# Modulation sums along rows on VectorE, and a start that follows the rows of h one by one, in a three-block transformer kernel

## What is computed

```
shift, scale, gate = split(c @ mod_w[layer, 0] + mod_b[layer, 0], 3)
h = rms_norm(x, norm_w[layer, 0, 0]) * (1 + scale) + shift
y = mixer(h)                         # or swiglu(h)
x = x + gate * rms_norm(y, norm_w[layer, 0, 1])
```

## Time and profile before

| | us |
|---|---|
| median of 3 runs | 1029.87 (1028.25 to 1030.72) |
| span of the profiled execution | 1029.8 |
| TensorE / VectorE / ScalarE busy in it | 987.3 / 792.3 / 559.9 |

### The profile page before, as it was taken

How to read it: one execution, slowest core, us unless ns; L and a number is a source line. 1 busy time by engine, 2 the same in 40 slices (tenths; PEclk the granted TensorE clock), 3 DMA queues, 4 the chain that set the end, 5 groups by cost and what they waited for, 6 DMA issues and landing times. The chain is left out here.

```text
span 1029.8 us, 21353 instructions
## 1 busy us (share of the span) xinstructions
PE 987.3 (96%) x8118; PEld 954.4 (93%) x8118; DVE 792.3 (77%) x1320; ACT 559.9 (54%) x1126; POOL 4.6 (0%) x14
## 2 busy tenths in 40 slices
PE   6999989999999999999999999999999999999996
PEld 5998768999999999989899999998989899999995
DVE  4758996788888777888788888876767857887775
ACT  2435774644444455574554444445657457666763
POOL 0100000000000000000000000000000000000000
PEclk9999999999999999999999999999999999999998
DMA  9995677488888656813558888774722425555431
GB/s 359 348 271 184 246 269 254 168 309 299 306 306 304 247 185 233 304 57 121 186 217 315 300 301 308 282 262 167 248 66 68 155 80 195 200 197 184 183 115 41
DMA packets 62569, 227.59 MB, mean 221 GB/s; under 512 B 7042, under 2 KB 7298, under 8 KB 62244
## 3 DMA queue, kind: packets, MB, share of 16 engines
q1 hardware_dynamic: 61716, 224.02, 60.5%
q0 software_dynamic: 640, 2.10, 0.9%
q10 hardware_dynamic: 144, 0.52, 0.1%
HBM read 225.04 MB, written 1.57 MB: 220 GB/s over the span
## 5 line engine op out<-in xcount | busy, mean ns | idle before, releaser
L1994 PE MATMUL bank<-hH,wH 128*128 128x258 f32 (+1 forms) x1544 | 444.2, 288 | 12.1 <-DVE hL L1343 8.4
L1995 PE MATMUL bank<-hL,wH 128*128 128x258 f32 (+1 forms) x1544 | 438.0, 284 | 0.0
L1996 PE MATMUL bank<-hH,wL 128*128 128x258 f32 (+1 forms) x1544 | 436.3, 283 | 0.0
L1278 DVE TENSOR_TENSOR wL<-raw,wH 128x1024 fp32r<-128x1024 f32 x270 | 327.9, 1220 | 43.9 <-ACT wH L813 42.8
L1994 PEld LDWEIGHTS bank<-hH,wH 128*128 128x128 f32 x1544 | 292.4, 189 | 20.0 <-issue 11.2
L813 ACT ACTIVATE wH<-raw 128x1024 fp32r<-128x1024 f32 x270 | 276.3, 1047 | 46.8 <-DMA raw<-in_weights 25.0
L1996 PEld LDWEIGHTS bank<-hH,wL 128*128 128x128 f32 x1544 | 293.6, 190 | 0.0
L1995 PEld LDWEIGHTS bank<-hL,wH 128*128 128x128 f32 x1544 | 293.1, 190 | 0.4
L1994 PE MATMUL bank<-aH,wH 128*128 128x256 f32 x592 | 169.2, 286 | 3.0 <-DVE wL L1278 3.0
L1996 PE MATMUL bank<-aH,wL 128*128 128x256 f32 x592 | 168.6, 285 | 0.0
L1995 PE MATMUL bank<-aL,wH 128*128 128x256 f32 x592 | 168.5, 285 | 0.0
(11 more groups left out here) (353 smaller groups left out, 1138.6 us busy)
## 6 DMA issues: line engine op xcount, KB each, us to landing
raw<-in_weights SPq DMA_DIRECT2D x270, 512.0 KB, 4.6
modbuf<-in_mod_w SPq DMA_DIRECT2D x69, 512.0 KB, 6.1
modbuf<-in_w_ada SPq DMA_DIRECT2D x36, 512.0 KB, 6.5
strips<-in_mod_w SPq DMA_DIRECT2D x16, 512.0 KB, 7.0
strips<-in_w_ada SPq DMA_DIRECT2D x12, 512.0 KB, 7.0
strips<-bias_table POOLq DMA_DIRECT2D x8, 256.0 KB, 6.8
raw<-in_mod_w SPq DMA_DIRECT2D x2, 512.0 KB, 4.2
otok<-in_mod_w SPq DMA_DIRECT2D x2, 512.0 KB, 9.8
```

The source lines that it names most:

```text
L1278: V.tensor_tensor(wL[:, slot, :], raw[:, slot, :], wH[:, slot, :].bitcast(F32), ALU.subtract).then_inc(lo_ready[c], 1)
L1994: mm(out, lhs_h, rhs_h, start=start, stop=False, skip_group_check=True)
L1995: mm(out, lhs_h, rhs_l, start=False, stop=False, skip_group_check=True)
L1996: return mm(out, lhs_l, rhs_h, start=False, stop=stop, skip_group_check=True)
```

## The change

- A matrix of a job is now laid out by output column: partition = output feature, 1024 input features along the row. `c` lies in `crow`, the same row on all 128 partitions. A job is one `tensor_tensor_reduce` on VectorE: product with `crow`, sum along the row, times a weight (the norm weight), starting from bias (times weight). Its result is one column of `mv`, `sc1` or `gw1`, ready for use. The start values of all columns are set in five small operations at the beginning. A second instruction per job reads the sum out.
- `mod_sum` and `mod_take` are gone, with their semaphores; users wait for a number of jobs (`wait_mods`). The accumulators are gone.
- `keep_clock` behind the norm sums is 18 matmuls in all four gaps (it was 3, 3, 6 and 3, beside 16, 16, 8 and 16 of sums).
- `silu(c_2)` is taken of the whole row, 128 x 1024, by ScalarE at the end of `f0`.
- In the start the order of SyncE is: parameters, first half of `x`, `crow`, second half, then matrices in pairs (scale and shift of row k), with units 0, 1 and 2 among them and unit 3 behind. `first_rows(k)`, `first_high(k)` and `first_low(k)` make row k of `h` once its two sums are there, and TensorE does `first_products` of units 0, 1, 2 for that row. Five of the eight shift sums stay on TensorE (`shift_product`), from matrices in the old layout. The gates come before `bc` and the values. The strips wait for the last row of `h`.
- The loops of SyncE and VectorE over steps of the feed-forward phases are written out.

```diff
+SHIFT, SCALE, GATE = range(3)
+MODS = [(0, part * KT + k) for k in range(KT) for part in (SCALE, SHIFT)]
+ON_TENSOR = [2 * k + 1 for k in (1, 3, 5, 6, 7)]
...
-            dst = acc[:, at:at + D]
-            cc = cvec[:, 0, :] if m < 4 else csil[:, :]
-            if d >= 1:
-                eng.wait_ge(mod_used, d)
-            if k == 0:
-                ops.tensor_scalar(dst, src, cc[:, 0:1], None, ALU.mult).then_inc(mod_used, 1)
-            else:
-                ops.scalar_tensor_tensor(out=dst, in0=src, scalar=cc[:, k:k + 1], in1=dst,
-                                         op0=ALU.mult, op1=ALU.add).then_inc(mod_used, 1)
...
+                weight = 1.0
+                if part == SCALE:
+                    weight = normw[:, 2 * m if m < 4 else 4 + m, k:k + 1]
+                elif part == GATE and m < 4:
+                    weight = normw[:, 2 * m + 1, k:k + 1]
+                total = (mv, sc1, gw1)[part][:, m, k:k + 1]
+                V.tensor_tensor_reduce(src, src, crow[:, m // 4, :], weight, total, ALU.mult, ALU.add,
+                                       total).then_inc(mod_used, 1)
...
+            for half in range(2):
+                ks = slice(half * KT // 2, (half + 1) * KT // 2)
+                sp.dma_start(x[:, ks, :], A["xT"][:, ks, :]).then_inc(x_landed[half], 16)
+                if half == 0:
+                    sp.dma_start(crow[:, 0, :], bass.AP(A["c"].tensor, 0, [[0, P], [1, D]])).then_inc(c_landed, 16)
+            load_start_job(0)
+            sp.dma_start(con[:, 0:CONST_FIRST], A["consts"][:, 0:CONST_FIRST]).then_inc(con_landed, 16)
+            load_start_job(1)
+            load_unit(0)
+            load_start_job(2)
+            load_start_job(3)
+            load_unit(1)
+            load_start_job(4)
+            load_start_job(5)
+            sp.dma_start(rel, A["rel"]).then_inc(rel_landed, 16)
+            load_start_job(6)
+            load_start_job(7)
+            load_unit(2)
+            for q in (8, 9, 10, 11, 12, 13, 15, 14):
                 load_start_job(q)
...
-            pool.wait_ge(misc_taken, misc["mod0h"] + 1)
+            pool.wait_ge(h_ready, KT)
...
                 if phase != "f2":
+                    shift_high(a)
                     split_high(base + 3 * FT + 2)
+                if phase == "f0":
+                    act.wait_ge(c_landed, 32)
+                    nc.scalar.activation(crow[:, 1, :], crow[:, 1, :], ACT.Silu).then_inc(csil_ready, 1)
                 nc.scalar.preload_act_table_set("natural_log_exp_and_others")
...
                 scaled(0)
-                if late != SHIFT_OF[a]:
-                    mod_take(late)
-                else:
-                    scaled(1)
-                    mod_take(late)
...
-            pe.wait_ge(misc_taken, misc["modA1"] + 1)
             norm_sums("B0")
-            mod_sum("modG0")
-            mod_sum("modS1")
-            keep_clock(bank[0], 3)
+            keep_clock(bank[0], 18)
             ffn("f0", 1)
             norm_sums("B1")
-            mod_sum("modG1")
-            mod_sum("modS2")
-            keep_clock(bank[4], 3)
+            keep_clock(bank[4], 18)
...
             pe.wait_ge(fw_ready, H)
-            mod_sum("modA3")
             turn_otok(1)
...
             pair_turn(0)
-            mod_sum("modA5")
             pair_scores(1)
...
+            first_products(0, (0,))
+            first_products(0, (1,))
+            first_products(1, (0, 1))
...
+            first_products(2, (0, 1, 2, 3))
+            for e in range(3):
+                first_products(e, (4,))
+            shift_product(11)
+            for e in range(3):
+                first_products(e, (5,))
+            shift_product(13)
+            for e in range(3):
+                first_products(e, (6,))
+            shift_product(15)
+            keep_clock(bank[2], 4)
+            for e in range(3):
+                first_products(e, (7,))
```

More of the change, by code:

```diff
@@ L1925, in _ @@
             copy_first(0)
-            mod_take("modA5")
             split_upto(base + 15)
@@ L1938, in _ @@
             pair_max(3)
-            mod_take("modG5")
             split_upto(base + 16)
@@ L2399, in ab_out @@
                 last.then_inc(unit_used[e % 3], 1)
-            first_pair(0, (bank[4], bank[5]), 0, S)
-            ab_project(2)
+            pe.wait_ge(hH_ready, KT)
+            pe.wait_ge(gw_ready, 2)
+            for k in range(KT):
+                last = three(bank[7][0:24, 0:S], gwH[:, k], gwL[:, k], hH[:, k, 0:S], hL[:, k, 0:S], k == 0, k == KT - 1)
+            last.then_inc(misc_psum, 1)
             pe.wait_ge(hot_landed, 16)
@@ L2410, in _ @@
             ab_values()
-            misc_free("gates")
-            pe.wait_ge(gw_ready, 2)
-            for k in range(KT):
-                last = three(bank[7][0:24, 0:S], gwH[:, k], gwL[:, k], hH[:, k, 0:S], hL[:, k, 0:S], k == 0, k == KT - 1)
-            last.then_inc(misc_psum, 1)
             ab_project(6)
```

573 lines of the change are left out of this document (225 added, 348 removed), and 4 rows, old and new, of the table MOD_COLUMNS.

## The result

The changed kernel takes 1042.25 us (median of 4 runs, 1039.33 to 1042.66); the kernel before took 1030.3 us beside it. The ratio is 1.0113, 95% interval 1.0089 to 1.0137. The forecast was 1017.2 us. The profiled run of the changed kernel is its shortest, 1039.33 us, with a span of 1037.5 us against 1029.8, so the traces have 7.7 us to explain. The medians are 12 us apart: the three other runs of the changed kernel are 2.7 to 3.3 us longer at a mean granted clock of 0.971 to 0.973, where the profiled one has 0.976, and they have no trace.

What follows compares the result with a forecast made beforehand. TensorE, busy for 96% of the span, was taken as the bound, so time is won where it waits or does needless work. 9.9 us behind the start plus 2.8 at the start make 12.7: 1029.9 to 1017.2 us, range 1009 to 1024.

Steps and rivals of the forecast that it cites:

- The start: Up to the scores: rows of h wait for two matrices each, so scores start at 65.7 instead of 68.50, 2.8 us won.
- 1.3 (job) + 0.5 (row) + 0.5 (high) + 0.5 (low): Start, last row of h: time from its matrix at 36.1 until the row is ready at 39.1 us, formerly 42.05.
- The clock: Start, rival that it gives nothing: at 1.2 GHz gates and bc take 4.7 us more; 1020 to 1025, 17%.
- What is late next is the transfer of unit 8: Start: ScalarE waits for unit 8 until 59.3 to 60.0, so only 2.8 of the 5.8 us lead is kept.
- The new instruction: VectorE's modulation jobs: tensor_tensor_reduce takes 1.28 to 1.34 us, against 0.66 us of slack per job, no cost in the loops.
- The rival of the doubled reduction: VectorE jobs: two SBUF sources double the instruction's time, costing 39 us in f0 and f1, some 10 in ab; about 1066, 6%.
- norm gaps, three and one: VectorE's chain after norms loses its mod_take: 1.35 us won in each of three gaps, 0.9 after cd, 4.95 in all.
- end of `f0`: Before f0's last down: ScalarE also gets the Silu of the second c ahead of the table load, 0.85 us lost.
- `cd`, transposes earlier: In cd, the 32 records of modA3 go and turn_otok starts when its input is ready, 1.25 us won.
- `sb`: Sums removed in sb: 2.5 us won from modA5, 0.4 from modG5, 0 from modG4.
- `modA5` term: In sb, 32 records on the chain before the row maximum go, but a 1.2 us VectorE split now stands there: 2.5 us won.
- hidden behind four splits: 0: In sb, removing modG4's sums wins nothing, because four splits on VectorE hide them.

Runs made afterwards that it cites:

- e1: Changed kernel with TensorE's five shift sums each issued one row earlier in its queue, with three PSUM banks for one; 1034.96 us.
- e3: Changed kernel with all 16 first sums on VectorE and none on TensorE; 1029.68 us.
- e8: Changed kernel with TensorE's five sums as matrices land, then all 72 products of the first three units; 4 fillers; 1031.01 us.
- e5: Changed kernel in its order, with keep_clock fillers no longer than the waits (15 before row 1's products, 5 for each 1.47 us wait); 1034.09 us.
- e10: Changed kernel with unit 8 loaded before SyncE's wait for the last row of h; 1038.24 us.
- e12: Start of e11 with two sums ahead of more products and more fillers, plus the three edits of e7, against the changed kernel; 1025.12 us.
- e7: Changed kernel plus 9 fillers before cd's transposes, two VectorE splits put later in sb, second c's Silu moved into f0's loop; 1037.81 us.
- e4: Like e8 against the changed kernel, but with 24 fillers in the place of 4; ratio to the kernel before 1.0057.
- e11: Changed kernel with recast start alone: sums as matrices land, rows 0 to 3's products between, fillers, earlier splits, constants and unit 8; 1023.2 us.

## Why the prediction was wrong, and where it was right

**The start** was forecast 2.8 us earlier at the scores and was 17.8 later. The step that failed is the sentence that puts the last row at its matrix (36.1) plus "1.3 (job) + 0.5 (row) + 0.5 (high) + 0.5 (low)", 39.1 us (the terms add up to 38.9). It treats TensorE as free when a sum's matrix lands. The order of the changed code, which I had before me, has each sum behind the products of the row before. e1 (6.1 us from order alone), e3 (9.9 us without TensorE in the path) and e8 (15.5 us with the sums ahead of all products) show it. The "9 matmuls are left where 72 were" was right, and the changed kernel does them from 59.86 to 61.95; but following the rows in this order is what made the rows late. The same sentence also treats VectorE as free, and that was wrong too: with TensorE's sums out of the way, in e8, the last job started 3.9 us behind the landing of its matrix and the row came at 44.1. The landing itself was put at 36.1 and was 37.7. In none of the twelve runs did the last row come before 43.2, or the scores before 69.7, behind the 68.5 of the kernel before. So the order is the larger error of this sentence, not the only one.

**The clock** stood among the rivals at 4.7 us and 17%, for gates and `bc` alone. e5 prices it at 6.7 to 8.0 us on the last row, as much as the order. By the row for 20 to 40 us it was low earlier than I allowed, where the table (3.78 us, 1.99 in e5) and a sum (3.51 for 1.90) lie on the circle. The listed sign, 1.2 GHz between 35 and 60 us, appeared. So this rival did happen; its size was taken from the wrong work.

**"What is late next is the transfer of unit 8"** failed as a reading of the earlier trace rows: a wait of 10.14 us on ScalarE, but TensorE was busy for 28.4 of the 29.1 us from 39.4 to 68.5. Scores follow values by 18.2 us in the kernel before, by 17.0 in the changed one and by 18.1 without that wait (e10), the last two with part of the stretch at half clock. The mechanism did appear in e12 (19.9 us), where the rest had become fast enough.

**The new instruction**: forecast 1.28 to 1.34 us, measured 1.278 to 1.339. The rival of the doubled reduction is out. VectorE in the loop of `f0`: 107.1 of 120 us, 89%, "under 90%" as forecast. By that rule of the Trainium skill (Vector Engine (DVE) Microarchitecture Reference, section 7), two fp32 sources in SBUF should have halved the throughput; this trace disagrees, with 1278 ns for what takes 1220 as a plain subtraction. (The section names the form `S2S2D2_STT`; the trace calls the instruction `CUSTOM_DVE_ANT_0`, and that the two are one family was my reading.)

**Behind the start** the sum of 9.9 us came out as 10.1, but partly by other terms:

| term | forecast | trace |
|---|---|---|
| norm gaps, three and one | 1.35 each and 0.9 | 1.62, 1.66, 1.62 and 1.20 |
| `ab` up to its norm | 1.35 | 0.8 |
| end of `f0` | -0.85 | -0.2 |
| `cd`, transposes earlier | 1.25 | 0.1 |
| end of `f1` | 0.25 | 0.5 |
| `sb` | 2.9 | 1.4 |
| `f2` and the end | 0 | 1.3 |

The norm gaps are read from `rstd` to `rstd`. Their chain on VectorE behind `f0` (answering):

```profile
392.37 0.69 DVE L1292 TENSOR_TENSOR otok<-bank,rstd 128x512 f32<-128x512 f32 x1 [1.85 <-ACT rstd L749]
393.09 0.88 DVE L1301 SCALAR_TENSOR_TENSOR x<-otok,gw,x 128x256 f32<-128x256 f32 x2
...
400.70 0.88 DVE L1259 SCALAR_TENSOR_TENSOR hL<-x,sc,hH 128x256 fp32r<-128x256 f32 x2 [0.18 <-ACT hH L786]
```

From 392.37 to 401.58 it is 9.21 us; forecast 9.3. The Silu stands where it was put, and the squares behind it end sooner than I had them (answering):

```profile
385.64 1.04 ACT L910 ACTIVATE crow<-crow 128x1024 f32<-128x1024 f32 x1
386.70 1.28 ACT L911 ACT_TABLE_LOAD   x1
388.00 1.08 ACT L758 ACTIVATE sq<-bank 128x512 f32<-128x512 f32 x2
388.97 1.09 ACT L758 ACTIVATE pr<-bank 128x512 f32<-128x512 f32 x2
```

From the end of the table load to the end of the squares it is 2.08 us; before it was 2.84, because the last two waited for TensorE. Taking the Silu away won 0.65 us in e7, so the term was of the right kind and its net size too large by 0.6.

In `cd` the gain was there and the clock took it back (e7). In `sb` the row maximum came 2.65 us earlier from the `modA5` term (forecast 2.5), but without `modG4` TensorE stood idle for 2.37 us before `attention_out` and went on at half clock; this is "hidden behind four splits: 0" turned round, since the 16 records had filled the idle time as well. Moving two splits made TensorE's operand 2.2 us earlier in e7 (VectorE's `hL` at 807.47 instead of 813.04, of which 3.3 is the shift of the whole run) and won only 0.15 in the stage: VectorE then does the same splits ahead of the norm. Ahead of the first row maximum `sb` also lost 0.6 us (37.8 us from `rstd` to it, formerly 37.2). How the 1.5 us missing in `sb` divide among these, I didn't separate, and the figure itself is soft: the changed kernel's code for `sb` took 106.5 to 110.1 us in ten traces, so the one with 106.7 is among the lucky ones.

The 1.3 us in `f2` were not foreseen, and most of them are not the change's. The kernel before runs at 0.52 of the clock from 1014 to 1021 us, with products of `f2` and the last norm in it. In the nine traces of changed kernels in which the clock stays full up to the last `rstd`, `f2` takes 193.2 us; in the four with a stretch at half clock there (e4, e8, e11, e12) it takes 193.7 to 194.3, with the same code, against 194.5 before. So 1.1 of the 1.3 us is the clock of one execution, and the 10.1 us behind the start come close to the forecast's 9.9 in part by luck.

## What to carry to other kernels

When work is taken from one engine and the rest of it stays there, place each remaining piece by what stands ahead of it in that engine's queue: a short sum behind work that waits for the previous result turns a pipeline into a circle, and the price is turns times the length of a turn. A long wait on one engine is on the path only if the engine that sets the end is idle at its end; look at that engine's busy time over the stretch first. When you forecast an event from the landing of its data, add what still stands in the queue of each engine that handles it. And "useless" matmuls before a wait may be what keeps the clock up: when they are removed, price the work behind the wait at half speed, or put in fillers no longer than the wait.

## What the runs showed of the hardware

- A reduction (`tensor_tensor_reduce`, 128x1024, both sources fp32 in SBUF) takes 1.278 us with an immediate weight, 1.339 with the weight from SBUF (1.319 in the group that mixes both), and its read 0.083, which overlaps the next. It is as dear as a multiply-add (1.280).
- The granted clock fell to 1.2 GHz in the middle of the program at idle times of 2.3 us (before 486.5 and 813.9 us), where before the change such stretches were filled. The same idle time doesn't always do it: at the one in `cd` (2.3 us) it fell, at once or within 1.4 us, in all ten traces without fillers, at the one of 3.0 us in `f2` in five of fourteen. So equal code differs by 1 to 3 us per stage from one execution to the next.
- Once down, it can stay down though TensorE is busy: in e1 TensorE is busy for all of 30 to 40 us and the granted clock is 0.50; the work there is sums of 64 columns, the table, and products of 256 columns.
- The same code up to the first `rstd` varied by 3 us between runs (16.9 to 19.8) with the landing of the constants (11.0 to 12.7), more than several of the effects looked for. Counting from the event behind it made the runs comparable to within 1.4 us.
